# Two-layer diffusion backbone on one core: output pair by rows, exchanges on SyncE, splits ahead of rotations

## The chip, the core and the metric
The kernel runs on one core of a Trainium2 chip. It is written by hand for the engines: TensorE (PE) multiplies, ScalarE (ACT), VectorE (DVE) and GpSimd (POOL) work on tiles in SBUF and PSUM, and SyncE (SP) issues most transfers. Each engine takes its instructions in the order written, and semaphores join them. The metric is the device time of one execution in microseconds; less is better.

## The reference, cut to what matters
Two layers over 512 latent tokens and 256 context tokens, width 1024, all in float32. A layer is a SwiGLU FFN (inner width 2816), token mixing, and a second FFN, each on RMS-normed and modulated tokens:

```python
h = h + 0.5 * m[2] * _swiglu(_modulate(_rmsnorm(h, ffn1_norm[i]), m[0], m[1]), ...)
n_lat = _modulate(_rmsnorm(h, mix_norm[i]), m[3], m[4])
# token mixing: p = n @ w_in, cut into pool | MLA | differential attention
#   q, k of the differential part are rotated:
#   _rope(x) = [x1 * c - x2 * s, x1 * s + x2 * c]
#   y = concat(pool, mla, diff) @ w_out
h = h + m[5] * y
h = h + 0.5 * m[8] * _swiglu(_modulate(_rmsnorm(h, ffn2_norm[i]), m[6], m[7]), ...)
```

The modulation vectors m come from a product of SiLU(c) with w_mod (1024 x 9216 a layer). In layer 1 the context is no longer carried past the mixing, so its FFN2 and parts of its projections are 512 tokens wide instead of 768. Output: the latent tokens after a last RMSNorm.

## The kernel before
**Products in three parts.** A float32 product is made of three reduced-precision ones: each weight tile and each activation tile is split into a high part (ACT casts it) and a low part (DVE subtracts the high part from the original). A *row* (`row`) is one 128-deep step k of a product: high x high, low activation x high weight, high activation x low weight, over all tokens. A *unit* is one output tile of 128 columns: 8 rows (11 in the FFN's second product). Units come in pairs, slot s = 0 and 1, each with its own weight tiles `raw_w`, `hi_w`, `lo_w` and its own PSUM tile `pair[s]`.

**Sweeps.** `plan_sweeps` lists the sweeps in their order. For a layer: FFN1 (up and down, twice), the input projection in pieces ("in" with arg 0, 4, 6, T_DQ = 8 for queries, T_DK = 12 for keys, T_DV = 16 for values), the output projection "out" (4 pairs), and FFN2. Each engine walks through this list by itself, in its own block; nothing but the order of the code and the waits decides who comes when.

**A unit's way.** SyncE loads the weights (`load_unit`) once `lo_ready[s]` says that the slot's last raw tile was split. ACT casts (`split_hi`, line 1039) once `unit_done[s]` says that TensorE no longer needs the old high part; DVE makes the low part (`split_lo`, line 1403); TensorE waits for it in `open_slot` (and for `pair_free[s]`, the reading out of the slot's PSUM tile), and multiplies (lines 694 and 700). `finish` on DVE then scales the result out of PSUM and on ACT adds the bias.

**Rotations.** For the 4 query and 4 key tiles (and the rotary key of the MLA part) `rope` on DVE needs a copy of the tile with its halves exchanged. `swap` makes it with four DMAs of 32 partitions; here ACT issues them (line 1172), at the end of its `finish` of the tile. The copies go to seven places `swapped` in `v_mla` and `v_tok`, of which two are used twice.

**Latent squares.** After "in" with arg 6 ACT squares the two KV tiles and the three Q tiles (`latent_squares`, lines 1047 and 1050), for the norms inside MLA. `latent_rstd` and `latent_apply` (line 1549, DVE) use them in the key sweep.

**From "out" to FFN2.** "out" reads its activations from `n_hi` and `n_lo`, 8 tiles of 768 columns. FFN2's first product reads its normed tiles from the same memory, laid out otherwise: for row k a block of 512 columns and, behind all blocks, a tail of 320. So ACT (`high`, line 1087) and DVE (`low`, line 1442) write no normed tile before the last unit of "out" is done (`unit_done` of both slots). Then `first_pair` on TensorE takes the first pair of FFN2 row by row as the tiles come (`n_ready`), with slot 1 four rows behind slot 0, and the sums of squares (`sum_stream`, lines 631 and 634) ahead of slot 1's first row. In layer 0 DVE also makes modulation sums (`mod_add`, lines 1572 and 1575) in the FFN sweeps, of `mod_w` loads of 1 MB.

## Time and profile before
| what | value |
|---|---|
| median of three runs | 2899.12 us (2898.11 to 2900.68) |
| the profiled execution's own time | 2900.54 us |
| its span in the trace | 2898.7 us |
| PE busy | 2824.4 us, 97% |
| DVE busy | 1667.3 us, 58% |
| ACT busy | 886.3 us, 31% |
| input projection, layer 0 / layer 1 | about 617 to 785 / 2156 to 2305 us |
| "out", layer 0 / layer 1 | about 956 to 1028.7 / 2446 to 2494.6 us |

The span is the program on the chip and the rest of the time lies around it. A busy share says little by itself: TensorE is busy nearly all the time, and what can be gained is in its short waits and in stretches at its lower clock (1.2 instead of 2.4 GHz; the profile gives the mean granted clock of a stretch as a share of the full one). A row of the timeline that ends in brackets shows how long the engine had been idle before it, and what it waited for.

### The profile page before, as it was taken

What the parts mean: (1) busy time and instruction counts of PE and PEld (TensorE: products, weight loads), DVE (VectorE), ACT (ScalarE), POOL (GpSimd) and SP (SyncE); (2) the same over time, 40 slices, a digit from 0 to 9 for tenths busy, and PEclk for the clock granted to TensorE, in tenths of its full rate; (3) what the DMA queues carried; (4) which work ended last, traced back from release to release, by engine and by line L of the source; (5) the groups of instructions that cost most, each with busy time, mean ns of one, the idle gap of its engine ahead of it and who ended that gap; (6) DMA issues with size and microseconds to landing.
All of it is one profiled execution on the core that took longest, in us unless ns stands there. A gap on an engine that the chain in (4) does not pass through costs nothing.

```text
span 2898.7 us, 43885 instructions
## 1 busy us (share of the span) xinstructions
PE 2824.4 (97%) x16954; PEld 2427.8 (84%) x16954; DVE 1667.3 (58%) x3117; ACT 886.3 (31%) x1370; POOL 105.8 (4%) x82
## 2 busy tenths in 40 slices
PE   6999999999999999999999999999999999999998
PEld 4888888888866888888888888888888866898996
DVE  5876588743567578757876435434344566443443
ACT  4221122233366342212222322122232366422232
POOL 0000000025000000000000000000015000000000
PEclk8999999999999999999999999999999999999999
DMA  6443344323300133433433223222223300233232
GB/s 227 122 132 115 111 123 128 119 58 87 90 8 1 37 112 120 131 116 116 123 120 91 58 65 113 68 65 61 74 59 97 96 2 8 81 93 102 87 98 69
DMA packets 425674, 259.63 MB, mean 90 GB/s; under 512 B 27073, under 2 KB 418857, under 8 KB 425578
## 3 DMA queue, kind: packets, MB, share of 16 engines
q1 hardware_dynamic: 421872, 253.87, 29.4%
q10 hardware_dynamic: 3706, 4.46, 0.6%
q8 instruction: 63, 1.03, 0.1%
q14 instruction: 33, 0.27, 0.0%
HBM read 251.88 MB, written 2.10 MB: 88 GB/s over the span
## 4 chain that ended last, share of the span: by engine, by line
PE 92%; DVE 3%; ACT 2%; issue 1%; ACTq 1%; DMA 0%; SPq 0%; DVEq 0%
PE pair L700 55%; PE pair L694 27%; PE pair L959 2%; PE pair L912 2%; PE pair L927 1%; PE pair L936 1%; PE pair L664 1%; PE pair L944 1%; PE pair L889 1%; ACTq L1172 1%; ACT hi_w L1039 1%; DVE lo_w L1403 1%; PE pair L877 0%; PE pair L882 0%; DMA x_tok<-in_ctx 0%
## 5 line engine op out<-in xcount | busy, mean ns | idle before, releaser
L700 PE MATMUL pair<-n_hi,hi_w 128*128 128x260 f32 (+2 forms) x3456 | 849.2, 326 | 23.5 <-DVE n_lo L1442 12.0
L700 PE MATMUL pair<-n_hi,lo_w 128*128 128x258 f32 (+2 forms) x3456 | 844.6, 325 | 0.0
L700 PE MATMUL pair<-n_lo,hi_w 128*128 128x256 f32 (+1 forms) x3456 | 843.9, 324 | 0.0
L700 PEld LDWEIGHTS pair<-n_hi,hi_w 128*128 128x128 f32 x3456 | 533.2, 189 | 88.0 <-DVE lo_w L1403 13.9
L700 PEld LDWEIGHTS pair<-n_hi,lo_w 128*128 128x128 f32 x3456 | 536.0, 190 | 57.5
L700 PEld LDWEIGHTS pair<-n_lo,hi_w 128*128 128x128 f32 x3456 | 534.9, 189 | 56.1
L1403 DVE TENSOR_TENSOR lo_w<-raw_w,hi_w 128x1024 fp32r<-128x1024 f32 (+1 forms) x296 | 394.3, 1332 | 318.7 <-ACT hi_w L1039 317.9
L1039 ACT CAST hi_w<-raw_w 128x1024 fp32r<-128x1024 f32 (+1 forms) x296 | 329.2, 1112 | 698.8 <-PE pair L700 368.3
L1575 DVE SCALAR_TENSOR_TENSOR mod_acc<-mod_w,silu_c,mod_acc 128x256 f32<-128x256 f32 x896 | 364.7, 479 | 0.0
L1498 DVE TENSOR_TENSOR buf<-pair,rstd 128x512 f32<-128x512 f32 (+1 forms) x308 | 164.9, 571 | 311.2 <-PE pair L700 311.1
L694 PE MATMUL pair<-h_hi,hi_w 128*128 128x512 f32 x1232 | 338.7, 345 | 0.0
L694 PE MATMUL pair<-h_lo,hi_w 128*128 128x512 f32 x1232 | 338.4, 344 | 0.0
L694 PE MATMUL pair<-h_hi,lo_w 128*128 128x512 f32 x1232 | 338.3, 344 | 0.0
L1526 DVE SCALAR_TENSOR_TENSOR x<-pair,gate,x 128x512 f32 (+3 forms) x136 | 82.0, 637 | 265.6 <-PE pair L694 265.5
L1136 ACT ACTIVATE buf<-buf,bias 128x512 f32<-128x512 f32 (+1 forms) x154 | 90.0, 625 | 462.3 <-DVE bias L1499 462.3
L694 PEld LDWEIGHTS pair<-h_hi,hi_w 128*128 128x128 f32 x1232 | 194.2, 188 | 30.3
L694 PEld LDWEIGHTS pair<-h_lo,hi_w 128*128 128x128 f32 x1232 | 194.4, 188 | 29.9
L694 PEld LDWEIGHTS pair<-h_hi,lo_w 128*128 128x128 f32 x1232 | 194.2, 188 | 29.9
L1141 ACT CAST h_hi<-buf 128x768 f32 (+3 forms) x88 | 68.9, 783 | 180.2 <-DVE buf L1504 180.2
L1262 ACT ACTIVATE buf<-pair,neg_max 128x768 f32<-128x768 f32 (+1 forms) x120 | 98.1, 818 | 64.8 <-DVE neg_max L1728 64.5
L1728 DVE TENSOR_REDUCE neg_max<-pair 128x1 f32<-128x768 f32 (+1 forms) x120 | 100.5, 842 | 23.2 <-PE pair L912 21.6
L1087 ACT ACTIVATE n_hi<-x,scale_a 128x256 fp32r<-128x256 f32 x136 | 57.9, 497 | 177.0 <-DVE x L1526 174.9
(185 smaller groups left out, 1926.5 us busy)
## 6 DMA issues: line engine op xcount, KB each, us to landing
raw_w<-in_ffn_w SPq DMA_DIRECT2D x176, 512.0 KB, 3.8
mod_w<-in_w_mod SPq DMA_DIRECT2D x64, 1024.0 KB, 5.1
raw_w<-in_ffn_w SPq DMA_DIRECT2D x64, 704.0 KB, 4.6
raw_w<-in_w_in SPq DMA_DIRECT2D x38, 512.0 KB, 3.9
raw_w<-in_w_out SPq DMA_DIRECT2D x16, 512.0 KB, 3.8
pro_scale<-in_w_mod SPq DMA_DIRECT2D x2, 2048.0 KB, 15.5
pro_shift<-in_w_mod SPq DMA_DIRECT2D x2, 2048.0 KB, 13.1
x_tok<-in_x SPq DMA_DIRECT2D x4, 512.0 KB, 5.8
```

Of the source, the lines that this page charges most:

```text
L694: mm = pe.matmul(pair[s][:, a:a + m], wt[:, k * P:(k + 1) * P], tile(src, k, m, a), start=opens, stop=closes)
L700: mm = pe.matmul(pair[s][:, a:a + m], wt[:, k * P:(k + 1) * P], src[:, of(k):of(k) + m], start=opens, stop=closes)
L912: mm = pe.matmul(pair[s][:, a:a + m], tile(proj, T_DQ + h, P, at)[rows_s, :], tile(proj, T_DK + h, m, k0 + a)[rows_s, :], start=True, stop ...
L1039: act.copy(hi_w[s][:, 0:w["kt"] * P], raw_w[s][:, 0:w["kt"] * P]).then_inc(hi_ready[s], 1)
L1136: ins = act.activation(act_buf[:, a:a + m], act_buf[:, a:a + m], ACT.Silu, bias=bias[0][:, e:e + 1])
L1141: act.copy(tile(h_hi, i, width(w, 1)), hid_buf[:, 0:width(w, 1)]).then_inc(hhi_ready, 1)
L1262: act.activation(buf[s if s < 2 else 3][:, 0:nk], pair[s][:, 0:nk], ACT.Exp, bias=neg_max[:, slot(c, s)], accum_out=exp_sum[:, slot(c, s)] ...
L1403: dve.tensor_tensor(lo_w[s][:, 0:m], raw_w[s][:, 0:m], hi_w[s][:, 0:m].bitcast(F32), ALU.subtract)\
L1498: dve.tensor_tensor(dst[:, a:a + m], src, rstd[:, a:a + m], ALU.mult)
L1526: ins = dve.scalar_tensor_tensor(out=xs, in0=pair[s][:, a:a + m], scalar=gate[:, bass.ds((2 * i + s) * 2 + e, 1)], in1=xs, op0=ALU.mult, o ...
L1575: ins = dve.scalar_tensor_tensor(out=acc, in0=part, scalar=gain, in1=acc, op0=ALU.mult, op1=ALU.add)
L1728: dve.tensor_reduce(neg_max[:, slot(c, s)], pair[s][:, 0:nk], AX.X, ALU.max, negate=True)\
```

## The change
Six things are moved; what is computed stays.

1. The exchanges (`swap`) are issued by SyncE instead of ACT. An exchange stands behind the load of the unit one sweep later, so that the first stands in the key sweep. The loads of the key and value sweeps are written out instead of looped.
2. `latent_squares` is cut in two and moved into the query sweep: the KV squares behind the cast for slot 1, the Q squares behind the cast of the next pair.
3. The rotations on DVE come one step later each, behind the split of the next weights instead of ahead of it. The last one (7) stands at the end of the value sweep.
4. The last pair of "out" (`last_pair`) takes its rows in the order 7, 6, 5, 0, 1, 2, 3, 4, slot 1 six rows behind slot 0. Each row that slot 1 has done raises `row_freed`.
5. ACT writes the normed tiles of FFN2 as `row_freed` lets it: the shift columns after 3 rows, tile 0 after 4, tiles 1 and 2 after 5, 3 after 6, 4 and 5 after 7, the last two after the whole pair. DVE makes the low parts of tiles 0 to 4 and only then finishes the last unit of "out". The cast for FFN2's first unit goes ahead of ACT's square of unit (3, 0).
6. `first_pair` puts the sums behind slot 1's first row.

```diff
+            def swap(L, j, s, n):
+
+                sp.wait_ge(in_done[s], n)
+                slot, half = SWAP_SLOT[j], (DDIM if j < 2 * HEADS else ROPE) // 2
+                if slot > 2:
+                    sp.wait_ge(pool_ready, 2 * (L + 1))
+                if slot in SWAP_SLOT[:j]:
+                    sp.wait_ge(roped, 2 * HEADS * L + SWAP_SLOT.index(slot) + 1)
+                elif L:
+                    sp.wait_ge(mla_out, N_PIECES[0])
+                lo, hi = (0, P) if j < 2 * HEADS else (NOPE, NOPE + ROPE)
+                for p in range(lo, hi, half):
+                    sp.dma_start(swapped[slot][p:p + half, :],
+                                  tile(proj, SWAPPED[j], SEQ)[p ^ half:(p ^ half) + half, :]).then_inc(swap_full[slot], 16)
+
+            def swap_of(w, i, s):
+
+                if w["what"] == "in" and w["arg"] >= T_DK:
+                    first = 0 if w["arg"] == T_DK else HEADS
+                    source = [v for v in SWEEPS if v["layer"] == w["layer"] and v["what"] == "in"
+                              and v["arg"] == (T_DQ if first == 0 else T_DK)][0]
+                    swap(w["layer"], first + 2 * i + s, s, units_before(source, "in") + i + 1)
...
                 if w["what"] != "out":
                     load_unit(w, 0, 0, True)
+                    swap_of(w, 0, 0)
                     load_unit(w, 0, 1, True)
+                    swap_of(w, 0, 1)
...
+                if w["what"] == "in" and w["arg"] >= T_DK:
+                    for s in range(2):
+                        load_unit(w, 1, s, False)
+                        swap_of(w, 1, s)
+                    if w["arg"] == T_DV:
+                        swap(w["layer"], 2 * HEADS, 1, N_IN * w["layer"] + IN_LATENT)
...
@@ -755,11 +792,11 @@
                         norm_row(n)
                         row(w, n, 0)
                     if n == LAG:
-                        if sums:
-                            sum_stream(sums)
                         open_slot(w, 0, 1, True)
                     if n >= LAG:
                         row(w, n - LAG, 1)
+                    if n == LAG:
+                        sum_stream(sums)
...
+            def last_pair(w):
+
+                ends = (LAST_ROWS[0], LAST_ROWS[-1])
+                open_slot(w, w["n"] - 1, 0, False)
+                for n in range(KD + LAST_LAG):
+                    if n < KD:
+                        row(w, LAST_ROWS[n], 0, ends=ends)
+                    if n == LAST_LAG:
+                        open_slot(w, w["n"] - 1, 1, False)
+                    if n >= LAST_LAG:
+                        mm = row(w, LAST_ROWS[n - LAST_LAG], 1, ends=ends)
+                        if n < KD + LAST_LAG - 1:
+                            mm.then_inc(row_freed, 1)
...
-                if w["n"] > 1:
-                    with pe.Fori(1, w["n"]) as i:
+                looped = w["n"] - (w["what"] == "out")
+                if looped > 1:
+                    with pe.Fori(1, looped) as i:
                         unit(w, i, 0, False)
                         unit(w, i, 1, False)
+                if w["what"] == "out":
+                    last_pair(w)
...
-            def latent_squares(L):
+            def latent_squares(L, g):
 
                 for s in range(2):
                     act.wait_ge(in_done[s], N_IN * L + IN_LATENT)
                 m = TOK if L < DEPTH - 1 else SEQ
-                for k in range(2):
-                    ins = act.activation(tile(proj, T_DV + k), tile(proj, T_KV + k), ACT.Square)
-                ins.then_inc(lat_sq, 1)
-                for k, dst in enumerate((tile(proj, T_DV + 2, m), tile(proj, T_DV + 3, m), sq[0][:, 0:m])):
-                    ins = act.activation(dst, tile(proj, T_Q + k, m), ACT.Square)
+                if g == 0:
+                    for k in range(2):
+                        ins = act.activation(tile(proj, T_DV + k), tile(proj, T_KV + k), ACT.Square)
+                else:
+                    for k, dst in enumerate((tile(proj, T_DV + 2, m), tile(proj, T_DV + 3, m), sq[0][:, 0:m])):
+                        ins = act.activation(dst, tile(proj, T_Q + k, m), ACT.Square)
                 ins.then_inc(lat_sq, 1)
...
-                        for s in range(2):
-                            act.wait_ge(unit_done[s], before["base"] + before["n"])
+                        freed = (KD - 1) * w["layer"]
+                        act.wait_ge(row_freed, freed + 3)
                         shift_high(w)
-                        high(0, w_cols)
-                        high(1, w_cols)
+                        for k, rows in enumerate((4, 5, 5, 6)):
+                            act.wait_ge(row_freed, freed + rows)
+                            high(k, w_cols)
                         split_hi(w, 0, 1, True)
+                        act.wait_ge(row_freed, freed + 7)
+                        high(4, w_cols)
+                        high(5, w_cols)
                         finish(before, before["n"] - 1, 1)
-                        act.wait_ge(pair_free[0], before["base"] + before["n"])
-                        for k in range(2, KD):
-                            high(k, w_cols)
+                        act.wait_ge(unit_done[1], before["base"] + before["n"])
+                        high(6, w_cols)
+                        high(7, w_cols)
...
-                    if w["arg"] in (T_DQ, T_DK):
-                        swap(w["layer"], (0 if w["arg"] == T_DQ else HEADS) + 2 * i + s, s,
-                             units_before(w, "in") + i + 1)
...
+                if w["what"] == "in" and w["arg"] == T_DQ:
+                    latent_squares(w["layer"], 0)
...
+                    if w["what"] == "in" and w["arg"] == T_DQ and i == 1:
+                        latent_squares(w["layer"], 1)
...
+                    if w["what"] == "out" and i == w["n"] - 1:
+                        split_hi(SWEEPS[q + 1], 0, 0, True)
...
-                if q + 1 < len(SWEEPS):
+                if q + 1 < len(SWEEPS) and w["what"] != "out":
                     split_hi(SWEEPS[q + 1], 0, 0, True)
...
                 if late_rows(w):
                     shift_low(w)
-                    low(0, w_cols)
-                    low(1, w_cols)
+                    for k in range(4):
+                        low(k, w_cols)
                 split_lo(w, 0, 1)
                 if late_rows(w):
-                    for k in range(2, KD):
+                    before = [v for v in SWEEPS if v["layer"] == w["layer"] and v["what"] == "out"][0]
+                    low(4, w_cols)
+                    finish(before, before["n"] - 1, 1)
+                    for k in range(5, KD):
...
+                if w["what"] == "in" and w["arg"] == T_DV:
+                    rope(w["layer"], 2)
...
                 if w["what"] == "in" and w["arg"] >= T_DK:
-                    L, j = w["layer"], w["arg"] - T_DK
-                    rope(L, j)
+                    L = w["layer"]
                     split_lo(w, 1, 0)
+                    if w["arg"] == T_DK:
+                        rope(L, 0)
+                    else:
+                        rope(L, 3)
+                        rope(L, 4)
                     finish(w, 0, 1)
-                    rope(L, j + 1)
                     split_lo(w, 1, 1)
                     if w["arg"] == T_DK:
                         latent_apply(L)
                     else:
-                        rope(L, j + 2)
+                        rope(L, 5)
                     finish(w, 1, 0)
-                    rope(L, j + (2 if w["arg"] == T_DK else 3))
...
                 if q + 1 < len(SWEEPS):
                     split_lo(SWEEPS[q + 1], 0, 0)
+                if w["what"] == "in" and w["arg"] >= T_DK:
+                    rope(w["layer"], 1 if w["arg"] == T_DK else 6)
                 if ends_step(w):
                     add_x(w["n"] - 1, 0, width(w, 0))
-                finish(w, w["n"] - 1, 1)
-                if w["what"] == "in" and w["arg"] == T_DK:
-                    rope(w["layer"], HEADS - 1)
+                if w["what"] != "out":
+                    finish(w, w["n"] - 1, 1)
+                if w["what"] == "in" and w["arg"] == T_DV:
+                    rope(w["layer"], 7)
```

SyncE at the start of the key sweep of layer 0, before. `raw_w0` and `raw_w1` are the two slots' weights, `v_tok<-k_cos_d` a table load, `v_mla<-proj` an exchange:

```order
L505 DMA raw_w0<-in_w_in 128x8x128
L505 DMA raw_w1<-in_w_in 128x8x128
L531 DMA v_tok<-k_cos_d 128x512
L531 DMA v_tok<-k_sin_d 128x512
L536 UNCONDITIONAL_BRANCH
L505 DMA raw_w0<-in_w_in 128x8x128
L505 DMA raw_w1<-in_w_in 128x8x128
```

and of the changed kernel:

```order
L508 DMA raw_w0<-in_w_in 128x8x128
L532 DMA v_mla<-proj 32x512 x4
L508 DMA raw_w1<-in_w_in 128x8x128
L532 DMA v_mla<-proj 32x512 x4
L559 DMA v_tok<-k_cos_d 128x512
L559 DMA v_tok<-k_sin_d 128x512
L508 DMA raw_w0<-in_w_in 128x8x128
L532 DMA v_mla<-proj 32x512 x4
L508 DMA raw_w1<-in_w_in 128x8x128
L532 DMA v_tok<-proj 32x512 x4
```

Four exchanges, 16 DMAs, now stand between the weight loads of this sweep, each behind one load and ahead of the next.

ACT around the query sweep of layer 0, before: casts (`hi_w`), finishes (`proj<-proj,bias`), squares (L1047, L1050) and an exchange (L1172):

```order
L1039 CAST hi_w0<-raw_w0 128x1024
L1153 ACTIVATE proj<-proj,bias1 128x512
L1153 ACTIVATE proj<-proj,bias1 128x256
L1047 ACTIVATE proj<-proj 128x768 x2
L1050 ACTIVATE proj<-proj 128x768 x2
L1050 ACTIVATE buf2<-proj 128x768
L1039 CAST hi_w1<-raw_w1 128x1024
L1153 ACTIVATE proj<-proj,bias0 128x512
L1153 ACTIVATE proj<-proj,bias0 128x256
L1172 DMA v_mla<-proj 32x512 x4
L1039 CAST hi_w0<-raw_w0 128x1024
```

and after, where L1102 and L1105 are the squares:

```order
L1093 CAST hi_w0<-raw_w0 128x1024
L1212 ACTIVATE proj<-proj,bias1 128x512
L1212 ACTIVATE proj<-proj,bias1 128x256
L1093 CAST hi_w1<-raw_w1 128x1024
L1102 ACTIVATE proj<-proj 128x768 x2
L1212 ACTIVATE proj<-proj,bias0 128x512
L1212 ACTIVATE proj<-proj,bias0 128x256
L1093 CAST hi_w0<-raw_w0 128x1024
L1105 ACTIVATE proj<-proj 128x768 x2
L1105 ACTIVATE buf2<-proj 128x768
```

The cast `hi_w1` moved ahead of the squares, and no DMA stands between a finish and the next cast.

DVE at the passage from "out" to FFN2 in layer 0, before: L1526 with `pair1` is the finish of the last unit, `n_lo` the low parts of the normed tiles (three instructions a tile), `mod_acc` the modulation sums:

```order
L1403 TENSOR_TENSOR lo_w0<-raw_w0,hi_w0 128x1024
L1414 TENSOR_TENSOR buf0<-buf0,buf2 128x768
L1526 SCALAR_TENSOR_TENSOR x<-pair1,gate,x 128x512
L1526 SCALAR_TENSOR_TENSOR x<-pair1,gate,x 128x256
L1435 TENSOR_TENSOR n_hi<-mod,n_hi 128x8x2
L1442 SCALAR_TENSOR_TENSOR n_lo<-x,scale_a,n_hi 128x256 x6
L1403 TENSOR_TENSOR lo_w1<-raw_w1,hi_w1 128x1024
L1442 SCALAR_TENSOR_TENSOR n_lo<-x,scale_a,n_hi 128x256 x18
L1572 TENSOR_SCALAR mod_acc<-mod_w,silu_c 128x256 x2
L1575 SCALAR_TENSOR_TENSOR mod_acc<-mod_w,silu_c,mod_acc 128x256 x14
```

and after, where L1572 is that finish:

```order
L1446 TENSOR_TENSOR lo_w0<-raw_w0,hi_w0 128x1024
L1457 TENSOR_TENSOR buf0<-buf0,buf2 128x768
L1478 TENSOR_TENSOR n_hi<-mod,n_hi 128x8x2
L1485 SCALAR_TENSOR_TENSOR n_lo<-x,scale_a,n_hi 128x256 x12
L1446 TENSOR_TENSOR lo_w1<-raw_w1,hi_w1 128x1024
L1485 SCALAR_TENSOR_TENSOR n_lo<-x,scale_a,n_hi 128x256 x3
L1572 SCALAR_TENSOR_TENSOR x<-pair1,gate,x 128x512
L1572 SCALAR_TENSOR_TENSOR x<-pair1,gate,x 128x256
L1485 SCALAR_TENSOR_TENSOR n_lo<-x,scale_a,n_hi 128x256 x9
L1618 TENSOR_SCALAR mod_acc<-mod_w,silu_c 128x256 x2
```

The finish moved from ahead of all normed tiles to behind the fifth, and the split `lo_w1` from behind the second to behind the fourth.

## Rows read from the trace of the kernel before
**Rows 1.** The page: the chain that ended last, share of the span by engine.
```profile
PE 92%; DVE 3%; ACT 2%; issue 1%; ACTq 1%; DMA 0%; SPq 0%; DVEq 0%
```

**Rows 2.** Timeline of PE, five waits: start us, us, engine, line, operation, count [idle].
```profile
687.24 0.62 PE L700 MATMUL pair<-n_hi,hi_w 128*128 128x512 f32 x2 [0.28 <-DVE lo_w L1403]
...
750.87 0.61 PE L700 MATMUL pair<-n_hi,hi_w 128*128 128x512 f32 x2 [2.15 <-DVE lo_w L1403]
...
2214.28 0.51 PE L700 MATMUL pair<-n_hi,hi_w 128*128 128x256 f32 x2 [2.09 <-DVE lo_w L1403]
...
2221.11 0.50 PE L700 MATMUL pair<-n_hi,hi_w 128*128 128x256 f32 x2 [0.85 <-DVE lo_w L1403]
...
2271.38 0.62 PE L700 MATMUL pair<-n_hi,hi_w 128*128 128x512 f32 x2 [1.35 <-DVE lo_w L1403]
```

**Rows 3.** Timeline of PE, both passages from out to FFN2.
```profile
1031.69 0.59 PE L700 MATMUL pair<-n_hi,hi_w 128*128 128x512 f32 x2 [2.95 <-DVE n_lo L1442]
...
1035.68 1.01 PE L700 MATMUL pair<-n_hi,hi_w 128*128 128x512 f32 x2 [0.80 <-DVE n_lo L1442]
...
2496.77 0.47 PE L700 MATMUL pair<-n_hi,hi_w 128*128 128x256 f32 x2 [2.15 <-DVE n_lo L1442]
...
2499.75 0.80 PE L700 MATMUL pair<-n_hi,hi_w 128*128 128x256 f32 x2 [0.57 <-DVE n_lo L1442]
```

**Rows 4.** Stretches: window, us, busy PE, PEld, DVE, ACT, POOL; PEclk; DMA; GB/s.
```profile
1028.00:1042.00 14.00, 10.25 (x39) 7.80 (x38) 12.49 (x30) 12.76 (x28) 0.00 (x0) 0.76 0.14 41
2494.00:2507.00 13.00, 10.28 (x48) 8.55 (x47) 8.60 (x19) 10.42 (x22) 0.00 (x0) 0.74 0.27 81
2207.00:2222.00 15.00, 12.05 (x99) 11.64 (x98) 5.08 (x11) 7.01 (x11) 7.98 (x6) 1.00 0.22 54
```

**Rows 5.** Timelines of ACT and DVE, query sweep, layer 1: cast, then split.
```profile
2225.25 1.05 ACT L1039 CAST hi_w<-raw_w 128x1024 fp32r<-128x1024 f32 x1 [2.57 <-issue]
...
2226.34 1.23 DVE L1403 TENSOR_TENSOR lo_w<-raw_w,hi_w 128x1024 fp32r<-128x1024 f32 x1 [4.41 <-ACT hi_w L1039]
```

**Rows 6.** Timeline of ACT, layer 1: first of the squares, and the cast.
```profile
2208.86 1.58 ACT L1047 ACTIVATE proj<-proj 128x768 f32<-128x768 f32 x2
...
2211.91 1.03 ACT L1039 CAST hi_w<-raw_w 128x1024 fp32r<-128x1024 f32 x1
```

**Rows 7.** The chain in order of time, output units: start us, us, what.
```profile
978.55 45.09 PE pair L694 x259
...
2460.62 30.99 PE pair L694 x132
```

**Rows 8.** Stretch with a finish and a rotation; timeline of DVE: latent_apply.
```profile
743.60:747.00 3.40, 3.40 (x21) 3.02 (x20) 3.08 (x7) 1.13 (x2) 0.00 (x0) 1.00 0.00 0
...
739.05 4.73 DVE L1549 SCALAR_TENSOR_TENSOR proj<-proj,gains,buf 128x768 f32<-128x768 f32 x5
```

**Rows 9.** DMA issues: out<-in, issuer, operation, count, KB each, us to landing.
```profile
mod_w<-in_w_mod SPq DMA_DIRECT2D x64, 1024.0 KB, 5.1
raw_w<-in_w_in SPq DMA_DIRECT2D x38, 512.0 KB, 3.9
...
v_mla<-proj ACTq DMA_DIRECT2D x32, 64.0 KB, 2.1
```

**Rows 10.** Splits into lo_w, 2160 to 2215 us: ns min/median/max, first, last.
```profile
L1403 DVE TENSOR_TENSOR lo_w<-raw_w,hi_w x8: 1225/1393/3928, 2162.3 to 2213.0; 128x1024 fp32r<-128x1024 f32 x8
```

**Rows 11.** Timeline of ACT: the last six normed tiles of each passage.
```profile
1033.02 7.27 ACT L1087 ACTIVATE n_hi<-x,scale_a 128x256 fp32r<-128x256 f32 x18
...
2497.88 4.88 ACT L1087 ACTIVATE n_hi<-x,scale_a 128x256 fp32r<-128x256 f32 x12
```

**Rows 12.** Timeline of DVE: modulation sums and the split for unit (1,1), layer 0.
```profile
1041.53 0.61 DVE L1572 TENSOR_SCALAR mod_acc<-mod_w,silu_c 128x256 f32<-128x256 f32 x2
...
1052.99 0.61 DVE L1572 TENSOR_SCALAR mod_acc<-mod_w,silu_c 128x256 f32<-128x256 f32 x2 [0.72 <-DMA mod_w<-in_w_mod]
...
1059.75 1.22 DVE L1403 TENSOR_TENSOR lo_w<-raw_w,hi_w 128x1024 fp32r<-128x1024 f32 x1
```

31 lines of the change are left out of this document (10 added, 21 removed).

## The prediction
> **What bounds the kernel now.** I began with the chain of work that ended last. TensorE holds 92% of it [rows 1], so only time in which TensorE stands still, or runs at its lower clock, can be won. Next I read TensorE's timeline for rows that end with an idle time in brackets, and kept those whose releaser the change touches. There are two kinds. In the projection sweeps TensorE waits for a weight tile's low part (DVE lo_w): 0.28 and 2.15 us in layer 0, then 2.09, 0.85 and 1.35 us in layer 1 [rows 2]; two more of the same kind, 0.54 and 0.53 us, follow the 0.85. At the passage from the output sweep to the second FFN it waits for the normed tiles (DVE n_lo): 2.95 and 0.80 us in layer 0, 2.15 and 0.57 us in layer 1 [rows 3]. Last came the granted clock in table by stretch: 0.76 over 14 us at the first passage and 0.74 over 13 us at the second, while it stays 1.00 around the 2.09 us stall [rows 4].
>
> **Part 1: the sweeps (swaps to SyncE, squares after the split, rotations after the splits).** What makes lo_w late is ACT. After a unit it finishes the tile, issues the four DMAs of an exchange, and only then casts the next weights: the cast follows 2.57 us of issuing, and DVE's split, which had waited 4.41 us, comes behind it [rows 5]. Taken off ACT, the cast comes some 2.57 us earlier, which is more than each of the stalls of 0.85, 0.54 and 0.53 us. The 0.28 and 2.09 us stalls stand behind latent_squares: from its start at 2208.86 to the cast at 2211.91 are 3.05 us [rows 6], and the cast now goes first. The 2.15 and 1.35 us stalls come in the key sweep behind one exchange of 2.57 us and then DVE's latent_apply and rotation. With the exchange gone from ACT, cast and split are 2.57 us earlier, more than either stall. A rotation (three DVE instructions) now always stands behind a split, not ahead of it. One row of work of a wide unit takes 45.09 / 259 x 6 = 1.045 us, so a unit is 8.36 us; in layer 1 a narrow row is 30.99 / 132 x 3 = 0.704 us and a unit 5.6 us [rows 7]. A finish and a rotation keep DVE busy for 3.1 us together and latent_apply for 4.7 [rows 8], a split for 1.2 [rows 5]. So a unit has at most 3.1 + 1.2 and a second rotation of about 2, or 1.1 + 1.2 + 4.7: 6.2 and 7.0 us, and both fit in 8.36. **Sum: 0.28 + 2.15 + 2.09 + 0.85 + 0.54 + 0.53 + 1.35 = 7.8 us.**
>
> What is late next? SyncE now has 18 exchanges between its weight loads. Each is queued behind the load of a unit and ahead of the load for the other slot, which is not asked for until half a pair (5.6 or 8.4 us) later; a load command, the 2.5 us of an exchange and the two table loads fit in that. Every exchanged tile was finished before the split that releases the load ahead of it, so in_done holds nothing. One wait is real: the last exchange needs rotation 3, some 4 us after the load for the output weights could start. That load then still has about 7 us before its cast and takes 3.9. An exchange lands 2.1 us after issue [rows 9] and DVE asks for it 20 us or more later. I cost all of it at nothing; should that cover go, a rival below prices it. The last rotation moves behind the last finish, where DVE has to wait for ACT's finish and cast, 1.1 and 1.0 us, anyway: nothing, at most 0.3 us.
>
> In layer 1 the moved split stands at about 2209.9, while GpSimd still works on the pooling. Eight splits there took 1.225 us at least, 1.393 in the middle and 3.928 at most [rows 10]. The worst would end at 2213.8, 1.6 us after its unit should start at 2212.2; the median does no harm. I take the median: 0, with 1.6 us kept for the range. The Trainium skill (SBUF — State Buffer, section Who interferes with whom) says that a VectorE instruction with two SBUF inputs and a GpSimd instruction that reads SBUF hold each other off, the later one being blocked to the end of the earlier; the trace agrees in so far as the long splits stand only in that stretch. By that rule the split waits out one pooling operation, whose length there would make the cost nothing.
>
> **Part 2: the passage, layer 0.** Let t = 0 be the start of the last output pair (1012.0); the pair is 16 rows, so it ends at 16.7. Rows of both units now alternate from the seventh on. The second unit's rows are freed after 11, 12, 13, 14 and 15 rows of work for counts 3 to 7. ACT takes 7.27 / 6 = 1.21 us a normed tile [rows 11], and DVE keeps step with it. ACT: tiles 0 to 3 end at 14.1, 15.3, 16.5 and 17.7 (the first waits for row 12, at 12.5 + 0.3), the cast at 18.7, tiles 4 and 5 at 19.9 and 21.1. DVE: low parts of 0 to 3 end at 15.3, 16.5, 17.7, 18.9, the split at 20.1, low part 4 at 21.4. TensorE goes straight on at 16.7, does tiles 0 to 3 until 20.9 and waits 0.5 us for tile 4. The finish of the last unit (1.1 us) and ACT's square follow; sums can start at 23.5, just as TensorE comes to them. Low parts 5 to 7 end at 23.7, 25.9 and 27.1, each ahead of its row. The first wait of 2.95 and the second of 0.80 us go, and with them the fall of the clock: 14.0 x (1 - 0.76) = 3.4 us of full clock were withheld, 0.4 of them while it stood idle anyway. So 3.75 + 3.0 - 0.5 = 6.25 us.
>
> Not all of it is kept, since DVE has the modulation sums right behind the tiles. They began at 1041.53 and the next load of mod_w came at 1052.99, with DVE waiting for that DMA; the split for unit (1,1) stood at 1059.75 and ended at 1060.97 [rows 12]. In the change low part 7 ends at 1012.0 + 27.1 = 1039.1, so all of this comes only 2.4 us earlier (the load takes 5.1 us in any case [rows 9]). The split then ends at 1058.6. TensorE needed it at 1063.4 before and would need it at 1057.1 now, so it waits 1.5 us. Afterwards DVE's 15.9 us of work per pair gain on TensorE's 16.7, and no more is lost. **Layer 0: 6.25 - 1.5 = 4.75 us.** Ends: 3 (the chain 1.5 us later than I drew it) and 6.3 (no DVE lag).
>
> **The passage, layer 1.** The same with a row of 0.704 us and 4.88 / 6 = 0.81 us a tile [rows 11]; cast and split keep their 1.03 and 1.22 us. Row 12 is free at 8.7, the pair ends at 11.3, low parts 0 to 3 end at 10.5 to 12.9, the split at 14.3, low part 4 at 15.2, while TensorE wants it at 14.1: 1.1 us. No modulation stands here. The waits were 2.72 us, and 13.0 x (1 - 0.74) = 3.4 us of clock, less 0.3 while idle, makes 3.1. **2.72 + 3.1 - 1.1 = 4.7 us**; ends 3 and 5.8.
>
> **Sum.** 7.8 + 4.75 + 4.7 = 17.2 us. The profiled execution took 2900.54 us with a span of 2898.7, so it goes to 2883.3. It is 1.4 us above the median of 2899.12; on the median the forecast is **2882 us** (-0.59%). With the ends of each term it runs from 2878 to 2887.
>
> **Rivals.**
> *The clock still falls.* The waits that stay (0.5, 1.5 and 1.1 us) or others keep costing. For it: a wait of 2.15 us was followed by a fall at one place [rows 3, 4]. Against it: 2.09 us was not [rows 4], and what stays is half as long. Two falls as large as now cost 3.0 + 3.1 us: 2888 us. The Trainium skill (TensorE: Matmul & The Clock Gate, section What's actually happening) says that activity releases the throttle and that the monitor runs on regardless of the kernel, so whether a given wait is caught also depends on where it falls. By that rule moving the program by 8 us reshuffles every fall, up as well as down: 2880 to 2888.
> *DVE is the new bound of the passage.* If low parts come 1.5 us later in each layer (ACT and DVE wait for one another tile by tile), each later use moves too: 2885 to 2888.
> *The early places don't help.* The tiles are not written earlier in effect, because ACT is held elsewhere. Then only Part 1 stays: 2899.1 - 7.8 = 2891.
> *Slower: SyncE becomes the bottleneck of the weights.* An exchange holds back the load behind it; in 16 of 18 cases that is a weight load. If each made TensorE wait its whole 2.5 us, 16 x 2.5 - 17.2 = 23 us: 2922 us. It decides once load command, exchange and landing (0.4 + 2.5 + 3.9 us or so) no longer fit between the split that releases the load and the next cast. Shortest such stretch: 6.0 us in layer 1, in which the exchange stands behind the load, not ahead.
>
> **Chances.** Forecast 0.62, clock 0.16, DVE 0.10, early places 0.05, SyncE slower 0.04, gains lost elsewhere to within 0.2% 0.03. About 0.2% (5.8 us) is what a measurement of this kernel tells from no change. The first four end below 2893.3, hence faster 0.93, same 0.03, slower 0.04. For eight in ten I take the ends of the terms, a clock luckier than now (2877) and the clock and DVE rivals: 2877 to 2889.
>
> **What would show it.** Right: no idle time before the first three tiles of ffn2_up, a granted clock near 1.00 in both passages, one short wait for n_lo at the fifth row, a wait of 1 to 2 us for lo_w some 28 us into ffn2_up of layer 0, no lo_w waits in the query, key and value sweeps, exchanges issued by SyncE and none by ACT. Wrong: casts that wait for raw_w, DVE waiting for an exchanged half, splits of 3 us at 2210, or a clock of 0.75 at either passage.

## The result and the profile after

| | before | changed |
|---|---|---|
| median | 2899.76 us (2898.11 to 2900.68, 4 runs) | 2881.07 us (2879.57 to 2886.91, 4 runs) |
| the profiled execution's own time | 2900.54 us | 2881.56 us |
| its span | 2898.7 us | 2879.7 us |

The ratio is 0.9942 (95% interval 0.9928 to 0.9955): 18.7 us less. The forecast was 2882 us.

The page of the changed kernel, the chain that ended last (before: [rows 1]):

```profile
PE 94%; DVE 3%; ACT 2%; issue 1%; DMA 1%; SPq 0%; DVEq 0%; ACTq 0%
```

Of the five waits of [rows 2] none is left. The stretches of the changed kernel, with the columns of [rows 4]: the sweeps of layer 0, the first passage, the sweeps of layer 1, the second passage.

```profile
640.00:785.00 145.00, 145.00 (x820) 125.55 (x819) 63.76 (x104) 44.66 (x63) 49.88 (x43) 1.00 0.32 79
1024.00:1038.00 14.00, 13.71 (x72) 10.97 (x71) 13.08 (x32) 12.57 (x23) 0.00 (x0) 1.00 0.13 37
2160.00:2290.00 130.00, 129.92 (x836) 117.44 (x835) 64.11 (x94) 40.71 (x55) 45.73 (x29) 1.00 0.36 91
2481.00:2494.00 13.00, 12.27 (x92) 11.10 (x92) 7.85 (x15) 11.50 (x17) 0.00 (x0) 1.00 0.15 44
```

TensorE is busy for 145.00 of 145 and 129.92 of 130 us in the sweeps, and the granted clock is 1.00 at both passages, where it was 0.76 and 0.74. Three waits are left at and behind the passages, in TensorE's timeline:

```profile
1029.34 0.62 PE L736 MATMUL pair<-n_hi,hi_w 128*128 128x512 f32 x2 [0.29 <-DVE n_lo L1485]
...
1054.64 0.62 PE L736 MATMUL pair<-n_hi,hi_w 128*128 128x512 f32 x2 [1.44 <-DVE lo_w L1446]
...
2483.85 0.51 PE L736 MATMUL pair<-n_hi,hi_w 128*128 128x256 f32 x2 [0.73 <-DVE n_lo L1485]
```

The 0.29 us stands where 2.95 and 0.80 us stood in [rows 3], the 0.73 us where 2.15 and 0.57 us stood; the 1.44 us is new. The exchanges are SyncE's. Its queue in the key sweep of layer 1 (raw_w is a weight load, v_mla<-proj x4 an exchange), which stands idle for 1.7 us between the second table load and the last weight load shown:

```profile
2214.31 0.38 SPq L508 DMA_DIRECT2D raw_w<-in_w_in  x1
2214.78 2.43 SPq L532 DMA_DIRECT2D v_mla<-proj  x4
2217.26 0.58 SPq L559 DMA_DIRECT2D v_tok<-k_cos_d  x1
2217.88 0.46 SPq L559 DMA_DIRECT2D v_tok<-k_sin_d  x1
2220.01 0.38 SPq L508 DMA_DIRECT2D raw_w<-in_w_in  x1
```

### Where the time went

I compare the start of the same cast in both traces (the casts are 296 in both, in the same order of units). ACT's timeline at the end of layer 0's sweeps and at the start and the end of layer 1's, the kernel before:

```profile
786.82 1.03 ACT L1039 CAST hi_w<-raw_w 128x1024 fp32r<-128x1024 f32 x1
...
2200.30 1.03 ACT L1039 CAST hi_w<-raw_w 128x1024 fp32r<-128x1024 f32 x1
...
2290.70 1.04 ACT L1039 CAST hi_w<-raw_w 128x1024 fp32r<-128x1024 f32 x1
```

and the changed kernel:

```profile
784.58 1.03 ACT L1093 CAST hi_w<-raw_w 128x1024 fp32r<-128x1024 f32 x1
...
2192.73 1.03 ACT L1093 CAST hi_w<-raw_w 128x1024 fp32r<-128x1024 f32 x1
...
2276.32 1.03 ACT L1093 CAST hi_w<-raw_w 128x1024 fp32r<-128x1024 f32 x1
```

The lead is 2.24, 7.57 and 14.38 us at these three places, so layer 1's sweeps alone brought 6.8 us. Done for every stage, also with a second profile of the changed kernel (the run `e5_after_again` below):

| stage | forecast | first profile | second profile |
|---|---|---|---|
| start of the program | 0 | -0.05 | 2.2 |
| first up sweep, layer 0 | 0 | -0.7 | 0 |
| sweeps, layer 0 | 2.4 | 3.0 | 3.0 |
| attention, layer 0 | 0 | 1.6 | 1.5 |
| passage and first up sweep behind it, layer 0 | 4.75 | 3.7 | 4.2 |
| sweeps, layer 1 | 5.4 | 6.8 | 6.8 |
| passage, layer 1 | 4.7 | 4.9 | 5.0 |
| the rest | 0 | -0.3 | -0.6 |
| sum | 17.2 | 19.0 | 22.1 |

The changed stages are the same in both profiles but for 0.5 us (in the first one 0.9 us is lost to a slower pace of the up sweep behind the passage, see below, and a wait there is 0.45 us shorter). What differs else between two executions of one kernel lies in stages that the change does not touch.

### The profile page after: what moved, and what is told of

The parts are those of the page before. It is cut to its first block, busy times and chain, and to the rows that moved or that the text cites. A ratio compares the mean times of both kernels' runs of the same rounds, so it can differ in the third digit from the quotient of the medians.

```text
span 2879.7 us, 43879 instructions
## 1 busy us (share of the span) xinstructions
PE 2816.0 (98%) x16954; PEld 2422.5 (84%) x16954; DVE 1669.2 (58%) x3117; ACT 884.3 (31%) x1370; POOL 106.4 (4%) x82
## 4 chain that ended last, share of the span: by engine, by line
PE 94%; DVE 3%; ACT 2%; issue 1%; DMA 1%; SPq 0%; DVEq 0%; ACTq 0%
PE pair L736 57%; PE pair L730 27%; PE pair L1013 2%; PE pair L966 1%; PE pair L981 1%; PE pair L990 1%; PE pair L698 1%; PE pair L998 1%; PE pair L943 1%; DVE n_lo L1485 0%; DVE mod_acc L1621 0%; DVE lo_w L1446 0%; PE pair L931 0%; PE pair L936 0%; DMA x_tok<-in_ctx 0%
## 5 line engine op out<-in xcount | busy, mean ns | idle before, releaser
L1572 DVE SCALAR_TENSOR_TENSOR x<-pair,gate,x 128x512 f32 (+3 forms) x136 | 82.0, 637 | 263.3 <-PE pair L730 263.1
```

Of the source, the lines that this page charges most:

```text
L1572: ins = dve.scalar_tensor_tensor(out=xs, in0=pair[s][:, a:a + m], scalar=gate[:, bass.ds((2 * i + s) * 2 + e, 1)], in1=xs, op0=ALU.mult, o ...
```

## The experiments

### Each half of the change alone

The kernel before with items 1 to 3 of the change (exchanges, squares, rotations):

```diff
                     load_unit(w, 0, 0, True)
+                    swap_of(w, 0, 0)
...
-                    rope(L, j)
                     split_lo(w, 1, 0)
+                    if w["arg"] == T_DK:
+                        rope(L, 0)
```

> The kernel before with the projection sweeps alone changed (exchanges on SyncE, squares cut and moved, rotations behind the splits); the last output pair, the normed tiles and the sums stay as before. If the idle times in brackets were the whole price of the stalls: 7.8 us less than before, 2892 us. If every stall costs some 0.27 us more than its bracket (distance from one matmul to the next less the usual distance; seven stalls): 9.7 us less, 2890 us. Rival: the gain of the sweeps needs the passage (no gain, 2900). If in this kernel too the short fall of the clock at 790 us is gone, 1.7 us less again. A pair of units in the first up sweeps of layer 0 should keep its 16.75 us, since nothing of TensorE's code ahead of them is touched.

Measured: 2889.85 us (5 runs) beside 2898.83 us of the kernel before: ratio 0.9963 (0.9949 to 0.9977), 9.0 us less. The leads in its sweeps are 3.0 and 6.8 us, just as in the whole change, so they do not need the passage. (The profile's whole span is 10.7 us shorter: as in the changed kernel, a short fall of the clock at the start of attention in layer 0 did not come in it, see below.) The price of a stall was read too low. TensorE's timeline of the kernel before around the 2.15 us stall of [rows 2]:

```profile
747.87 0.51 PE L700 MATMUL pair<-n_lo,hi_w 128*128 128x512 f32 x2
748.21 0.51 PE L700 MATMUL pair<-n_hi,lo_w 128*128 128x512 f32 x2
...
751.32 0.51 PE L700 MATMUL pair<-n_lo,hi_w 128*128 128x512 f32 x2
```

A group of two matmuls starts 0.35 us after the last one. Over the stall it starts at 750.87, which is 2.66 us after 748.21, and the next one after it 0.45 us later. The stall costs (2.66 - 0.35) + (0.45 - 0.35) = 2.41 us, 0.26 more than its bracket. I call this extra a refill; what makes it was not looked into. With 0.27 us for each of the seven stalls, an estimate from this one and its like, the sweeps come to 7.8 + 1.9 = 9.7 us, and 3.0 + 6.8 = 9.8 were measured. The run takes the exchanges, the squares and the rotations together; which of the three closed which stall was not tried. That the pace of the up sweeps would stay was wrong; see below.

The kernel before with items 4 to 6 (the last pair by rows, early tiles, late finish, sums later):

```diff
+                if w["what"] == "out":
+                    last_pair(w)
...
-                        for s in range(2):
-                            act.wait_ge(unit_done[s], before["base"] + before["n"])
+                        act.wait_ge(row_freed, freed + 3)
```

> The kernel before with the passage alone changed (last output pair by rows, normed tiles early, finish of the last unit late, sums behind slot 1's first row); the projection sweeps stay as before. My theory: both passages give what they gave together, 4.7 + 4.9 us, the stall for lo_w of some 1.4 us in layer 0 included, and the two up sweeps of layer 0 lose 0.1 us a pair, 1.8 us in all: 2892 us. If the slower pace had to do with the sweeps' change: 2890. Rival (the early places need the earlier ACT of the sweeps): over 2895.

Measured: 2891.15 us (10 runs), ratio 0.9978 (0.9969 to 0.9988), 7.7 us less. The passages show 0.29 and 0.71 us as in the whole change, and a lo_w wait of 1.19. The rival (over 2895) fell. Together the halves give 9.0 + 7.7 = 16.7 us, the whole 18.7; the difference is no larger than what single executions scatter. In the profile of e2 the two passages, with the up sweep behind the first, give 4.9 and 5.0 us; 1.1 us is lost in the sweeps of layer 1, which it does not touch and in which the clock fell once.

### The pace of the up sweeps

In the first profile of the changed kernel a pair of units took 16.85 us in the first up sweep of layer 0, where the kernel before took 16.75. The same cast of two pairs on ACT, changed kernel, first profile:

```profile
138.53 1.05 ACT L1093 CAST hi_w<-raw_w 128x1024 fp32r<-128x1024 f32 x1 [5.29 <-PE pair L736]
...
155.38 1.05 ACT L1093 CAST hi_w<-raw_w 128x1024 fp32r<-128x1024 f32 x1 [5.29 <-PE pair L736]
```

Of the code ahead of this loop only the place of the sums was changed. So I put the sums back in the changed kernel, and moved them alone in the kernel before:

```diff
                     if n == LAG:
+                        if sums:
+                            sum_stream(sums)
                         open_slot(w, 0, 1, True)
...
-                    if n == LAG:
-                        sum_stream(sums)
```

> The changed kernel, but TensorE's sums of squares again ahead of slot 1's first row. In the changed kernel a pair of units takes 16.85 us in the first up sweeps of layer 0 where it took 16.75 before, with the same instructions in the loop. Theory one: the place of the sums just ahead sets this pace; then both sweeps are back at 16.75 and the kernel is 1.8 us faster than the changed one, less what the sums wait for: 2879 to 2881. Theory two: the pace has another cause (the last pair written out, or the data of a run): pairs stay at 16.85 and the time at 2881 or somewhat more.

> The kernel before with one edit: the sums of squares stand behind slot 1's first row. Theory one (the place of the sums sets the pace of the loop behind it): the two up sweeps of layer 0 take 16.85 us a pair, 1.8 us more, 2901.5. Theory two: 16.75 us a pair and 2899.8.

Measured: 2883.18 us (4 runs, 2880.22 to 2885.17) and 2899.42 us (10 runs, ratio 1.000, 0.999 to 1.001). In e3 the first of the two sweeps had 16.75 and the other 16.85 us a pair, in e4 both had 16.75, and e1, whose TensorE code is that of the kernel before, had 16.85 in both. These three ran on one chip. My theory fell. Then the changed kernel as it is, once more:

> The changed kernel once more, with nothing edited. Is the pace of the layer-0 up sweeps (16.75 or 16.85 us a pair) a property of the program or of the execution? If of the execution, this profile may show another pair of paces than the first (16.85 and 16.85), and the median stays at 2881 with single runs from 2878 to 2887; if of the program, the same paces as before. The residual stalls should repeat: 0.29 us (n_lo) and 1.44 us (lo_w) in layer 0, 0.73 us in layer 1.

Measured: 2879.49 us (4 runs, 2878.47 to 2881.71), ratio 0.9933 (0.9917 to 0.995). Its profile has 16.75 us in both sweeps, with the same program. The same casts there:

```profile
136.20 1.06 ACT L1093 CAST hi_w<-raw_w 128x1024 fp32r<-128x1024 f32 x1 [5.24 <-PE pair L736]
...
152.95 1.06 ACT L1093 CAST hi_w<-raw_w 128x1024 fp32r<-128x1024 f32 x1 [5.24 <-PE pair L736]
```

So the program does not set the pace, nor does the chip: it belongs to the execution, and a sweep keeps one of two values from its start to its end. Of the 28 such sweeps in the 14 profiles seven had the slower one. What sets it stays open. It is worth 0.7 to 1.0 us a sweep.

### VectorE behind the first passage

```diff
-MOD_CUT = 6
+MOD_CUT = 4
```

> The changed kernel with four instead of six eighths of the modulation sums ahead of the split for slot 1. My theory (VectorE's modulation sums, begun only behind the normed tiles, make the split for unit (1,1) of the second up sweep late): four eighths less sums are four instructions of 0.48 us, 1.9 us, so the stall of 1.44 us and its refill of 0.27 go: 1.7 us less than the changed kernel, 2879.4. Rival (the split waits for ScalarE's cast or the weights): the stall stays, 2881. Rival two: the sums now delay the reading out of slot 0, and every pair becomes longer: over 2883.

Measured: 2879.37 us (4 runs), beside 2879.49 us of the unedited kernel in the same set. The wait for unit (1,1), 1.44 us in the first profile and 1.89 in the second, is 0.26 us, so it did stand behind the modulation sums; but a new one of 0.62 us comes one unit later. TensorE's timeline of e6:

```profile
1051.81 0.62 PE L736 MATMUL pair<-n_hi,hi_w 128*128 128x512 f32 x2 [0.26 <-DVE lo_w L1446]
...
1061.13 0.61 PE L736 MATMUL pair<-n_hi,hi_w 128*128 128x512 f32 x2 [0.62 <-DVE lo_w L1446]
```

The sums that were taken from ahead of one split stand ahead of the next. So 1.0 us of 1.89 was won, less a second refill, too little to see in the median. Rival two (every pair longer) did not come.

### What brings the tiles forward

```diff
-LAST_LAG = 6
+LAST_LAG = 8
```

> The changed kernel with the last output pair one unit after the other (slot 1 eight rows behind slot 0 instead of six), rows in the same order. By my count of rows (second unit's rows freed after 11, 12, 13, 14, 15 rows of work for counts 3 to 7) nothing changes, since with either lag slot 0 is through before the third row of slot 1: 2881, the same stalls of 0.3 and 0.7 us. Rival: the interleaving itself brings the tiles forward; then the stalls at the passage grow by two rows, 2 us in layer 0 and 1.4 us in layer 1: 2884 or more.

Measured: 2879.14 us (4 runs), and the same stalls of 0.29 and 0.73 us to the hundredth. The interleaving of the two slots brings nothing for the tiles. What is left is the order of the rows with the count `row_freed`, and the next run takes the early places away:

```diff
-                        for k, rows in enumerate((4, 5, 5, 6)):
+                        for k, rows in enumerate((7, 7, 7, 7)):
```

> The changed kernel, but ScalarE writes the first four normed tiles only after seven rows of slot 1 instead of after 4, 5, 5 and 6. My theory (the early places are what closes the passage): tile 0 starts after 15 instead of 12 rows, so TensorE waits 3 us more in layer 0 (1.5 for tile 0, the rest for tile 4) and 2.3 us more in layer 1, about 5.3 us and some refills, 2887, with a chance of falls of the clock on top, 3.4 us each. Rival (the rest of the reordering does it, the finish of the last unit behind tile 4 above all): 2881 to 2882.

Measured: 2885.33 us (4 runs), 5.8 us more than the unedited kernel in the same set. TensorE's timeline, both passages:

```profile
1024.15 0.58 PE L736 MATMUL pair<-n_hi,hi_w 128*128 128x512 f32 x2 [1.76 <-DVE n_lo L1485]
...
1029.98 0.62 PE L736 MATMUL pair<-n_hi,hi_w 128*128 128x512 f32 x2 [1.01 <-DVE n_lo L1485]
...
2481.54 0.48 PE L736 MATMUL pair<-n_hi,hi_w 128*128 128x256 f32 x2 [1.30 <-DVE n_lo L1485]
...
2485.93 0.51 PE L736 MATMUL pair<-n_hi,hi_w 128*128 128x256 f32 x2 [1.10 <-DVE n_lo L1485]
```

5.17 us of waits instead of 1.02, and two refills more: 4.7 us, and the spans differ by 5.0 (against `e5_after_again`). Of the 3.1 us by which tile 0 is held back in layer 0, 2.5 show as waits. So the early places bring about 5 of the 9.2 us of the two passages. The other 4 stay without them: no wait at the passages is over 1.76 us, and the clock falls at neither (see below). The late finish of the last output unit was not tried by itself.

### The room on SyncE

```diff
                 for p in range(lo, hi, half):
+                    for c in (0, SEQ // 2):
...
-                dve.wait_ge(swap_full[slot], per * L + at)
+                dve.wait_ge(swap_full[slot], 2 * (per * L + at))
```

> The changed kernel with every exchange cut into eight transfers of half the size instead of four: SyncE issues 16 x 4 + 2 x 2 = 68 more, some 2.5 us more per exchange, 5 us in all where the shortest stretch free for it was 4.4 us in layer 0 and about 2 to 4 us in layer 1. My theory (the exchanges are covered because there is room between two weight loads): some loads of layer 1's key sweep are issued up to 2 us later, but have several us to spare before their casts, so 2881 to 2882 and at most one short lo_w wait. Rival (each exchange delays the load behind it and TensorE pays): 16 x 2.5 us less the spare time, 2890 to 2920.

Measured: 2881.94 us (4 runs). SyncE is now full at the worst place, with nothing free between two exchanges of layer 1:

```profile
2209.43 4.99 SPq L533 DMA_DIRECT2D v_mla<-proj  x8
2214.46 0.58 SPq L508 DMA_DIRECT2D raw_w<-in_w_in  x1
2215.14 4.96 SPq L533 DMA_DIRECT2D v_mla<-proj  x8
2220.15 0.58 SPq L561 DMA_DIRECT2D v_tok<-k_cos_d  x1
2220.78 0.43 SPq L561 DMA_DIRECT2D v_tok<-k_sin_d  x1
2221.25 0.43 SPq L508 DMA_DIRECT2D raw_w<-in_w_in  x1
```

and yet TensorE does not wait in the sweeps (e9, columns of [rows 4]):

```profile
630.00:785.00 155.00, 155.00 (x879) 134.35 (x878) 66.53 (x108) 48.36 (x68) 58.19 (x47) 1.00 0.32 80
2160.00:2290.00 130.00, 129.91 (x834) 117.42 (x834) 64.13 (x94) 40.72 (x55) 45.30 (x28) 1.00 0.35 91
```

Twice the issuing costs nothing in the sweeps: the slower rival (2922 us) was far from deciding. Behind the sweeps of layer 1 a wait for the loads of wk_n is 2.90 us in this profile and 1.66 in the changed kernel's (1.55 to 1.66 in the other 13), though they were issued at the same distance. The fall of the clock there lasts twice as long as in the changed kernel, a second one follows, and the profile loses 4.1 us between the sweeps and "out" of layer 1. Whether the exchanges have to do with it stays open, so the run shows room on SyncE in the sweeps alone.

### What is left at the passages

The kernel with MOD_CUT = 4 and tile 4 ahead of the split:

```diff
-                        split_hi(w, 0, 1, True)
                         act.wait_ge(row_freed, freed + 7)
                         high(4, w_cols)
+                        split_hi(w, 0, 1, True)
...
-                    for k in range(4):
+                    for k in range(5):
                         low(k, w_cols)
                 split_lo(w, 0, 1)
...
-                    low(4, w_cols)
```

> The changed kernel with four eighths of the modulation sums ahead of slot 1's split, and with normed tile 4 ahead of the first unit's split for slot 1 on ScalarE and VectorE. My theory: of the stalls that are left at the passages (0.29 and 0.73 us for tile 4, each with 0.27 of refill) most goes, since tile 4 no longer stands behind a cast of 1.0 and a split of 1.2 us; slot 1's weights come about 0.9 us later than now, which is still 0.5 us or less behind TensorE's need: 1.0 us less from this, 1.7 from the sums, 2878.4. Rival: the stall moves to lo_w of slot 1 and is as long: 2879.4.

Measured: 2877.73 us (4 runs), ratio 0.9929 (0.9913 to 0.9946). The stalls for tile 4 went, but others took their place. TensorE's timeline of e10:

```profile
1029.43 0.58 PE L736 MATMUL pair<-n_hi,hi_w 128*128 128x512 f32 x2 [0.40 <-DVE x L1571]
...
2480.84 0.49 PE L736 MATMUL pair<-n_hi,hi_w 128*128 128x256 f32 x2 [0.77 <-DVE x L1571]
```

L1571 is the finish of the last output unit. I took it that the sums wait for it. The same timeline speaks against that: the row that waits is slot 1's first, and the sums (L665) come only behind it:

```profile
1030.55 1.02 PE L665 MATMUL pair<-buf,ones 128*128 128x512 f32 x2
```

The edit moved the sums:

```diff
-                    if n == LAG:
+                    if n == LAG + 1:
                         sum_stream(sums)
```

> The kernel of e10_tile4_first with the sums of squares one row later (behind slot 1's second row). There the stalls at the passages (0.40 and 0.77 us) were no longer for tile 4 but for the finish of the last output unit, which the sums read. My theory: one row of each slot more, 2.1 and 1.4 us, covers it: 0.40 + 0.77 and two refills of 0.27, 1.7 us less than e10: 2876. Rival: the norm factors come later by as much, so that the reading out of the first unit is late and TensorE waits for the place in PSUM at the next pair: no gain, 2877.7.

Measured: 2879.64 us (5 runs). Both stalls stayed to the hundredth. TensorE's timeline of e11:

```profile
1029.86 0.58 PE L736 MATMUL pair<-n_hi,hi_w 128*128 128x512 f32 x2 [0.40 <-DVE x L1571]
...
2482.28 0.48 PE L736 MATMUL pair<-n_hi,hi_w 128*128 128x256 f32 x2 [0.77 <-DVE x L1571]
```

The median is 1.9 us above that of e10; no stall at the passages or behind them grew by more than 0.04 us, but the clock fell twice for a short time in this profile (at 786 and 2424 us), and not in that of e10. The theory fell: TensorE waits in `open_slot` for the PSUM place of slot 1, which the same finish frees. That left VectorE's work ahead of it:

```diff
-            def low(k, w_cols):
+            def low(k, w_cols, cut=None):
...
+                    m = min(m, cut or m)
...
-                    for k in range(5):
-                        low(k, w_cols)
-                split_lo(w, 0, 1)
+                    for k in range(4):
+                        low(k, w_cols, 8 if k in (2, 3) else None)
...
                     finish(before, before["n"] - 1, 1)
+                    low(4, w_cols)
+                split_lo(w, 0, 1)
```

> The kernel of e10_tile4_first with less work on VectorE at the passages: the low parts of normed tiles 2 and 3 are made for 8 columns of each block only (the rest of them is left out), and the finish of the last output unit stands ahead of tile 4's low part. In e11 the stalls of 0.40 and 0.77 us stayed when the sums moved, so TensorE waits there for the PSUM place of slot 1, which that finish frees, not for the sums. My theory: what is left is VectorE's work from the first tile to that finish and the split. With 2.2 us (layer 0) and 1.5 us (layer 1) of it gone, the split ends at or before TensorE's need in layer 0 and 0.1 us after it in layer 1: no stall over 0.15 us at either passage, 0.40 + 0.77 and refills of 0.54, 1.7 us less than e10. Rival: ScalarE's chain of normed tiles and casts is the floor, and the stalls stay as they are, then on lo_w.

Measured: 2875.7 us (4 runs), ratio 0.9922 (0.9906 to 0.9939), 2.0 us less than e10; the kernel leaves out most of two tiles' low parts, so its result is not whole. TensorE has no stall at either passage (e12, columns of [rows 4]):

```profile
1024.00:1038.00 14.00, 14.00 (x75) 11.57 (x74) 13.75 (x34) 11.39 (x19) 0.00 (x0) 1.00 0.13 37
2477.00:2490.00 13.00, 12.98 (x99) 11.81 (x98) 6.96 (x15) 11.24 (x16) 0.00 (x0) 1.00 0.24 66
```

So what the change leaves at the passages is VectorE's work between the first tile and the opening of slot 1. This run took work away and put the finish earlier at once, so it does not say how much of it each did. Of the kernels that compute everything, e10 has the lowest median, 2877.73 us beside 2880.16 us of the changed kernel over its eight runs. By the stalls only about 0.5 us of that is accounted for, so I don't call it faster.

### The clock

No run was made for the clock alone; the profiles of all runs (14, two of them of the changed kernel) were read for it. At the passages three profiles have the old stalls of 2.95 and 2.15 us (before, e1, e4), and in all three the clock falls to its lower level at both, though in e4 only half as long at the first (0.88 over the 14 us instead of 0.76). In the other eleven, with stalls of 1.76 us at most, it falls at neither. So the 1.76 and 1.01 us of e8 brought no fall.

In the sweeps a stall of the same length sometimes brings a fall. The kernel before (first two rows) and e4, which has the same sweeps (last two), around the stalls of 2.15 and 2.09 us, columns of [rows 4]:

```profile
750.00:756.00 6.00, 5.13 (x29) 4.54 (x30) 3.71 (x7) 1.59 (x3) 0.00 (x0) 1.00 0.47 120
2212.00:2219.00 7.00, 4.91 (x41) 4.72 (x40) 2.40 (x4) 1.91 (x3) 3.29 (x2) 1.00 0.43 104
```

```profile
750.00:756.00 6.00, 5.89 (x25) 5.12 (x26) 3.08 (x8) 2.18 (x3) 0.00 (x0) 0.72 0.53 131
2210.00:2217.00 7.00, 5.25 (x31) 5.25 (x32) 2.39 (x4) 1.92 (x3) 2.76 (x2) 0.76 0.45 113
```

A fall there withholds 6.0 x (1 - 0.72) = 1.7 us of full clock. Of the three profiles with these two stalls (before, e2, e4), the first brought a fall in one, the second in two. A stall of 1.97 us at the start of attention (before, at 790.05), which the change does not touch, brought one in 4 of 14 profiles: in that of the kernel before, and in neither of the changed kernel's. That is the 1.5 to 1.6 us of the attention row in the table.

In the attention of layer 1, which the change does not touch either, one fall went and another came. The kernel before, and then the changed kernel:

```profile
2335.00:2341.00 6.00, 5.11 (x19) 2.66 (x18) 4.24 (x7) 2.87 (x6) 0.00 (x0) 0.72 0.01 3
```

```profile
2294.00:2300.00 6.00, 4.34 (x15) 3.43 (x14) 3.80 (x5) 2.76 (x6) 0.00 (x0) 0.72 0.92 215
```

The second follows the stall of 1.66 us for wk_n, which is 1.62 us in the kernel before and brought no fall there; in `e5_after_again` 1.55 us brought it again. So a short stall is no assurance: that e8's 1.76 us brought no fall is shown for that one profile.

## Why the prediction was right, point by point

**The sweeps.** The mechanism was right: casts and splits earlier by the issuing of an exchange, all seven stalls gone, nothing new. The term of 7.8 us was too small, measured 9.8. The step at fault is taking the idle time in brackets for the price of a stall; some 0.27 us a stall have to be added.

**SyncE at nothing.** Right, and with room: double the issuing did not reach TensorE in the sweeps (e9). An exchange lands 3.6 us after issue instead of the 2.1 of [rows 9], which nobody waits for.

**The split amid the pooling at nothing.** Right. Eight splits there took 1.225 to 3.908 us with 1.636 in the middle, more than the 1.393 of [rows 10]; the moved one, at 2202.2, took 1.756. TensorE waited only for the first of them, 1.20 us, as before the change (1.19).

**The passage, layer 0.** The first four tiles come without a wait, as drawn. The fifth waits 0.29 us (forecast 0.5), the split for unit (1,1) is late by 1.44 and 1.89 us (forecast 1.5), both where they were to stand. e6 shows that the second stands behind the modulation sums. Measured 4.2 us at the pace of the kernel before, forecast 4.75.

**The passage, layer 1.** 0.73 us of wait instead of 1.1, and 5.0 us instead of 4.7. I named tile 4 as the last thing late. e10 to e12 show that this was half of it: with tile 4 earlier, slot 1's place in PSUM is late by nearly as much, since both stand in one queue on VectorE.

**The clock.** The sum counted both falls as gone, 6.1 us, and both are gone. The rival (the clock still falls) did not happen at the passages. The Trainium skill (TensorE: Matmul & The Clock Gate, section What's actually happening) has the monitor run on regardless of the kernel; the traces agree in so far as the same stall brought a fall in one profile and none in the next. The rival that moving the program by 8 us reshuffles every fall came true in part: the falls in attention were dealt anew (one less in layer 0, one exchanged for another in layer 1), those at the passages were not. Whether the move or the execution dealt them is not told apart: the kernel before has one profile.

**The sum.** 17.2 us forecast, 18.7 measured in the medians. The first profile's 19.0 us is made of changed stages of about 19.3 us (at equal pace), of the fall of the clock at the start of attention that the kernel before happened to have (1.6), and of the slower pace in two sweeps of the changed kernel (-1.6 or so). Of the changed stages the sweeps were forecast 2.0 us too small and the second passage 0.2, the first passage 0.5 too large. So 2882 against 2881.07 is closer than the working deserves: the changed kernel's second set had 2879.49. Two small slips stand in the working. 3.1 + 1.2 + 2 is 6.3 us, not 6.2, which changes nothing. And the ends of the terms reach down to 2899.1 - (7.8 + 6.3 + 5.8) = 2879.2 us, not 2878, so the second set lies only just inside them.

**The early places** (the rival that only Part 1 stays, 2891): e8 shows that a delay of the tiles costs nearly its length, so they matter. But without them the time was 2885.33, not 2891: they are worth about 5 us, not all of Part 2.

## What to carry to other kernels

Price a stall of TensorE by the distance between the matmuls around it less the usual distance, not by the idle time in the timeline; here one of 2.15 us was 0.26 us dearer, and 0.27 us for each of seven accounts for the sweeps. Before a small effect is explained, look at a second profile of the same program: the start, the pace of a loop and single falls of the clock moved by up to 3 us here without an edit. And where a wait names an instruction, ask which of its results the waiting engine needs, and look at which instruction waits: the same finish fed the sums and freed the PSUM place. Moving the sums told which it was, and the order of the rows in the timeline could have told it without a run.

## What I had not expected of the hardware

- A loop of TensorE over the same 96 matmuls runs at 16.75 or 16.85 us a pair, for a whole sweep, and takes the one or the other in different executions of one program. What decides stays open.
- A stall of about 2 us brings a fall of the clock in some executions and not in others: at one place 1.97 us did in 4 of 14 profiles, at another (wk_n, layer 1) 1.55 to 1.66 us did in 3 of 13, while one of 1.87 us in attention (layer 0) brought it in all 14.
- The exchanges of 64 KB land 3.6 us after issue when SyncE sends them behind a weight load of 512 KB, and 2.1 us when ACT sent them. It was not tried whether the load ahead or the queue does this.
